# Half of an attention unit's dense products moved ahead of its turning

## The reference

```python
z = h @ w_in[l]
g_a, g_b, z_uv, z_q, z_k, z_v = jnp.split(z, COL_SPLITS, axis=-1)
y_a = gmlp_chunk_mixer(z_uv, ...)
y_b = diff_attention(q, k, v, positions, ...)
m = jax.nn.sigmoid(g_a) * (y_a @ a_w_proj[l]) + jax.nn.sigmoid(g_b) * (y_b @ b_w_proj[l])
x = x + m @ w_out[l]
```

```python
s = jnp.einsum('bhmqd,bhmkd->bhmqk', qb, kb)      # m: two maps per head, 64 features each
p = jax.nn.softmax(jnp.where(mask, s, -jnp.inf), axis=-1)
a = p[:, :, 0] - lam * p[:, :, 1]
o = jnp.einsum('bhqk,bhkd->bhqd', a, vf)
```

## Time and profile before

| | |
|---|---|
| time, median of 3 runs | 1990.88 us (1988.44 to 1991.02) |
| the profiled execution | 1990.19 us, its span 1988.5 us |
| TensorE busy | 1876.0 us, 94% |
| VectorE busy | 1132.6 us, 57% |
| ScalarE busy | 770.1 us, 39% |
| GpSimd busy | 273.7 us, 14% |

### The profile page before, as it was taken

How to read it: one execution, slowest core, us unless ns; L and a number is a source line. 1 busy time by engine, 2 the same in 40 slices (tenths; PEclk the granted TensorE clock), 3 DMA queues, 4 the chain that set the end, 5 groups by cost and what they waited for, 6 DMA issues and landing times.

```text
span 1988.5 us, 22680 instructions
## 1 busy us (share of the span) xinstructions
PE 1876.0 (94%) x8169; PEld 1445.1 (73%) x8169; DVE 1132.6 (57%) x1442; ACT 770.1 (39%) x1081; POOL 273.7 (14%) x246
## 2 busy tenths in 40 slices
PE   6999999989999999998999999897788989999998
PEld 4888888868886767776888888685333768888887
DVE  6556436454655554648767433448998555655532
ACT  4222222233345857214435222334234345445422
POOL 3111001110000000022100000222765300000000
PEclk8999999989999999999999999999998989999999
DMA  5555323333221111224634322342110222232222
GB/s 188 198 173 169 121 64 103 93 111 100 92 85 47 66 59 64 77 93 154 205 127 156 125 76 89 104 122 85 53 53 22 65 80 88 92 98 79 87 87 85
DMA packets 161896, 200.58 MB, mean 101 GB/s; under 512 B 7104, under 2 KB 136490, under 8 KB 161834
## 3 DMA queue, kind: packets, MB, share of 16 engines
q1 hardware_dynamic: 148714, 163.02, 25.6%
q0 software_dynamic: 8672, 28.33, 4.4%
q10 hardware_dynamic: 4448, 8.41, 1.1%
HBM read 189.24 MB, written 10.50 MB: 100 GB/s over the span
## 4 chain that ended last, share of the span: by engine, by line
PE 85%; DVE 10%; ACT 2%; issue 2%; DMA 0%; POOL 0%; DVEq 0%; POOLq 0%; ACTq 0%
PE bank L1671 40%; PE bank L1638 33%; PE bank L1854 6%; DVE sc_a L1520 2%; PE bank L1613 1%; DVE tmp L1028 1%; PE bank L1878 1%; DVE sc_v L1529 1%; PE bank L1650 1%; PE bank L1763 1%; DVE tmp L1541 1%; DVE sc_p L1541 1%; PE bank L2070 1%; DVE sc_p L1540 1%; ACT w_hi L616 0%
## 5 line engine op out<-in xcount | busy, mean ns | idle before, releaser
L1012 DVE TENSOR_TENSOR w_lo<-w_raw,w_hi 128x2048 fp32r<-128x2048 f32 x152 | 359.1, 2362 | 472.5 <-ACT w_hi L616 472.3
L616 ACT CAST w_hi<-w_raw 128x2048 fp32r<-128x2048 f32 x158 | 301.4, 1908 | 752.3 <-PE bank L1638 364.8
L1671 PE MATMUL bank<-h_hi,w_hi 128*128 128x512 f32 x1120 | 448.9, 401 | 35.4 <-ACT h_hi L639 17.6
L1671 PE MATMUL bank<-h_hi,w_lo 128*128 128x512 f32 x1120 | 445.9, 398 | 0.0
L1671 PE MATMUL bank<-h_lo,w_hi 128*128 128x512 f32 x1120 | 355.2, 398 | 0.0
L1671 PEld LDWEIGHTS bank<-h_hi,w_hi 128*128 128x128 f32 x1120 | 212.7, 190 | 90.3 <-issue 38.8
L1671 PEld LDWEIGHTS bank<-h_lo,w_hi 128*128 128x128 f32 x1120 | 212.3, 190 | 51.4
L1671 PEld LDWEIGHTS bank<-h_hi,w_lo 128*128 128x128 f32 x1120 | 212.9, 190 | 50.4 <-issue 0.2
L1638 PE MATMUL bank<-hid_hi,w_lo 128*128 128x512 f32 x528 | 208.8, 396 | 0.0
L1638 PE MATMUL bank<-hid_hi,w_hi 128*128 128x512 f32 x528 | 208.8, 396 | 0.0
L1638 PE MATMUL bank<-hid_lo,w_hi 128*128 128x512 f32 x528 | 208.8, 396 | 0.0
(11 more groups left out here) (368 smaller groups left out, 2644.6 us busy)
## 6 DMA issues: line engine op xcount, KB each, us to landing
w_raw<-in_w_in SPq DMA_DIRECT2D x29, 1024.0 KB, 5.1
mod_raw<-in_w_mod POOLq DMA_DIRECT2D x96, 256.0 KB, 3.6
w_raw<-in_ffn_w_gate SPq DMA_DIRECT2D x22, 1024.0 KB, 7.0
w_raw<-in_ffn_w_up SPq DMA_DIRECT2D x22, 1024.0 KB, 5.4
w_raw<-in_w_up SPq DMA_DIRECT2D x22, 1024.0 KB, 5.1
w_raw<-in_ffn_w_down SPq DMA_DIRECT2D x16, 768.0 KB, 4.7
w_raw<-in_ffn_w_down SPq DMA_DIRECT2D x16, 640.0 KB, 4.3
w_raw<-in_w_out SPq DMA_DIRECT2D x8, 1024.0 KB, 5.1
```

Source lines behind the costliest of these rows:

```text
L616: act.copy(w_hi[i % 2][:], w_raw[i % 2][:]).then_inc(S("w_hi_done"), 1)
L1012: dve.tensor_tensor(w_lo[s][:], w_raw[s][:], w_hi[s][:].bitcast(F32), ALU.subtract).then_inc(S("w_split"), 1)
L1671: mm = pe.matmul(bank[:], w[:, k, at], h[:, k, :], start=k == first and part == 0 and i == 0, stop=k == last and part == 1)
```

## The change

Of the 14 products of a step, seven are taken between `scores(u + 2)` and `weigh(u)`, and seven stay behind `values(u - 1)`. Nothing else is touched; `PER_UNIT` is still 14, and the other engines' lists are the same.

```diff
             for u in range(len(UNITS)):
                 if u + 2 < len(UNITS):
                     scores(u + 2)
+                beside(PER_UNIT // 2)
                 weigh(u)
                 if u:
                     values(u - 1)
-                beside(PER_UNIT)
+                beside(PER_UNIT // 2)
             values(len(UNITS) - 1)
             beside(480 - PER_UNIT * len(UNITS))
```

## The result

The changed kernel takes 1993.53 us (median of 15 runs, 1992.16 to 1994.97), the kernel before 1990.15 us (15 runs, 1988.02 to 1992.43) beside it. The ratio is 1.0018, with a 95% interval of 1.001 to 1.0025: slower by 3.4 us, and by less than 0.2% in the ratio. The prediction was 1993.8 us, from 1989.0 to 1997.3, with 0.73 on "within 0.2%".

The account below looks back on a forecast made before the run. TensorE, busy 94% of the span, was taken to bound the kernel. Waits gone -1.3, new stalls +3.3 and edge +0.9 made +2.9 us: 1993.1 for the profiled execution, 1993.8 against the median, range 1989.0 to 1997.3.

Parts of the forecast that it names:

- the edge: Switch from the mask's short matmuls to a product, 30 times: 0.03 us each, +0.9, with ends -0.9 and +2.4.
- turning of step 22: Step 22's `weigh` waits for VectorE's late weighted difference; products in front cover the wait, -1.14 us.
- turning of step 19: Step 19's `weigh` starts 0.28 us after the mask instead of 0.12; this smaller wait goes, -0.16 us.
- tile 4, step 17: `a_proj` tile starting at product 2 of step 17: its existing stall of 1.09 us grows by 0.37.
- tile 5, step 18: `a_proj` tile starting at product 0 of step 18: its existing stall of 0.34 us grows by 0.70.
- tile 3, step 16: `a_proj` tile starting at product 4 of step 16: new stall of 0.87 us for the multiply freeing its bank.
- tile 1, step 14: `a_proj` tile starting at product 8 of step 14: new stall of about 1.3 us for ScalarE's delayed sigmoid.
- tiles 2 and 6: `a_proj` tiles that come out within 0.1 us of their banks' release; 0.1 us put for both.
- R1: Only step 22's covered stall counts, banks come free early enough: -1.3, 1989.6 us; chance 0.12.
- R2: Each block behind the mask pays its first weight load; decides from 0.067 us a step, 1995.3 at 0.08; chance 0.15.
- R3: Stalls from 692 to 714 us lower TensorE's clock: one fall makes 1995.4 us, two 1997.0; chance 0.08.
- Nothing outside the stretch should move: From step 0's first scores to the last product about 3 us longer; nothing outside that should move.

Follow-up runs that it names:

- products behind the turning: Kernel before, with seven products between `weigh(u)` and `values(u - 1)` and seven behind the values; 1994.74 us in a single run.
- quiet steps: Kernel before, seven products moved ahead of `weigh(u)` only in steps 0 to 12, 20, 21 and 23 to 29, which have no stall; 1989.93 us, single run.
- all 14 ahead: Kernel before, with all 14 products of a step ahead of `weigh(u)` and none behind the values; 2002.87 us in a single run.
- products ahead of the mask: Kernel before, seven products between the scores' four matmuls and the mask's two, in steps 0 to 12, 20, 21, 23 to 29; 1996.28 us, single run.
- emptied first with step 22 split: Kernel before, VectorE's bank-emptying multiplications ahead of `row_max`, and seven products ahead of the turning in step 22 alone; 1987.03 us, ratio 0.9987.
- both engines first: Changed kernel, VectorE's multiplications ahead of `row_max` and ScalarE's sigmoid ahead of the next panel's cast; 1992.26 us, ratio 1.0012.
- before, emptied first: Kernel before, with only VectorE's bank-emptying multiplications moved ahead of `row_max`, TensorE's order unchanged; 1986.44 us, ratio 0.9983.

## Why the prediction was right

Its sum was -1.3 + 3.3 + 0.9 = +2.9 us, and the stretch lost 3.07. The mechanism is borne out term by term; that the sum comes as near as 0.2 us is in part luck, since single terms are off by up to 0.3, upward and downward. Taking the edge of 0.04 out of each step, the terms stand like this:

| term | predicted | from the steps |
|---|---|---|
| turning of step 22 | -1.14 | -1.34 |
| turning of step 19 | -0.16 | -0.20 |
| tile 4, step 17 | +0.37 | +0.40 |
| tile 5, step 18 | +0.70 | +0.72 |
| tile 3, step 16 | +0.87 | +0.94 |
| tile 1, step 14 | +1.3 | +1.18 |
| tiles 2 and 6 | +0.1 | +0.19 (tile 2 alone) |
| the edge, 30 steps | +0.9 (0.03 each) | +1.2 (0.04 each) |

- *The turnings.* Both waits went, and the kernel that splits only steps 19 and 22 shows that they don't return. The size was read from the bracket, 1.14, which counts from the modelled end of the mask matmuls. TensorE's timeline of the kernel before:

```profile
733.43 0.28 PE L1880 MATMUL bank<-mask_parts 128*128 128x128 bf16 x2
734.85 0.55 PE L1889 MATMUL bank<-ident,tmp 128*128 128x128 f32 x3 [1.14 <-DVE tmp L1361]
```

  From the mask to the turning it is 1.42 us where 0.12 is usual, so the wait cost 1.3, as the step's length says.
- *The releases.* That the multiplication is tied to the scores is shown by the reordering on VectorE, which takes all of these waits away, in the old order of TensorE and in the new. That a stall grows by the work that has left the place between scores and tile is borne out by the products behind the turning, where the stalls of tiles 4 and 5 grow less, each by the expected amount and the 0.08 that is not given back.
- *The detour through ScalarE.* A stall in step 14 from a turning in step 13 is shown by splitting step 13 alone. The subtraction of the cast's own wait was needed: without it the stall would have been put at 1.6.
- *The edge* was the term of the sum that was mis-sized, by 0.3 us in all. I started from the values edge, which is free, and put 0.03 where the quiet steps measured 0.04. The Trainium skill ("TensorE: Matmul & The Clock Gate", its part on LDWEIGHTS), with 107 ns for a weight load, gave an estimate of 0.04 a step. But the same account doesn't give the 0.10 behind the scores, nor the nothing behind values and turnings, so that its number fits shows no mechanism; the measurement decides.
- *The rivals.* R1 (only the cover counts) failed at the tiles. R2 (the edge decides) was off: 0.04 where it needed 0.067. R3 (the clock) did not come true: 1.00 was granted from 640 to 790 us, with waits up to 1.50 us. (Its "0.9 to 1.6 us" was a slip: the prediction's own terms make 1.46 at most.) With 3.33 us of waiting the clock did fall, in the run with all 14 ahead.
- *Nothing outside the stretch should move:* behind it nothing did; ahead of it the trace is 0.5 us shorter, within what that part varies from trace to trace.

The loss is 3.4 to 3.6 us by the runs and 3.07 in the stretch of one trace. The difference is within the runs' spread.

## What to carry to other kernels

Before filling a wait with work, add up the waits of that kind in the stretch: here 1.3 us in 170, and the move paid for them in every one of 30 steps. A product that is moved nearer to the start of a step is also moved nearer to the release of its own bank, and a result that is made later holds up whatever stands behind its reader in the reader's queue, a step further on. Where an engine empties a bank that the bound engine waits for, put that ahead of the instruction that itself waits for the bound engine: this one reordering on VectorE gained 0.17%, and the same idea on ScalarE lost, because another engine was waiting for what it pushed back.

## What the hardware showed

- A block of 128x512 products (0.233 us each) starts with a spacing of 0.31 to 0.34 us. After 128x128 fp32 matmuls (turnings or values) these are 0.08 shorter in sum and the block costs nothing; after the bf16 mask pair it costs 0.04 us, after the four fp32 matmuls with 64 rows about 0.10. Why is not shown.
- The idle time in a bracket is too small. It counts from the modelled end of the matmul before, and the first spacing behind a wait is longer (0.31 to 0.34 us for a product instead of 0.233): the turning's 1.14 us cost 1.3, and a wait under 0.2 us (tile 6 in step 18, products behind the turning) shows in no bracket.
- TensorE's clock stayed at 1.00 through waits of 1.50 us (changed kernel) and 2.08 us (all 14 ahead, 725 to 730 us above), and fell to 0.50, its level of 1.2 GHz, behind 3.33 us. Behind the 2.78 us of the kernel with products ahead of the mask it fell too, by its stretches:

```profile
735.00:740.00 5.00, 2.22 (x14) 1.96 (x11) 4.79 (x11) 0.77 (x4) 0.00 (x0) 0.75 0.40 125
740.00:745.00 5.00, 5.00 (x21) 3.52 (x21) 0.08 (x1) 3.20 (x9) 0.00 (x0) 0.91 0.26 89
```

  Two shorter waits close together did it as well. Behind the attention TensorE waits 2.19 and then 2.37 us, with a few transposes between and ahead of them, and in the kernel before its stretches are:

```profile
796.00:798.00 2.00, 0.73 (x4) 0.71 (x4) 2.00 (x4) 0.71 (x2) 0.00 (x0) 0.56 0.37 106
798.00:800.00 2.00, 1.16 (x4) 0.71 (x3) 2.00 (x4) 0.76 (x2) 0.00 (x0) 0.50 1.06 377
```

- Step 0, which begins at a reduced clock, took 5.9 to 6.1 us in nine of the profiled executions and 7.26 to 7.29 in three (products behind the turning; emptied first with step 22 split; both engines first). The second of them has in step 0 the same orders as "before, emptied first", which took 6.00, so a difference of 1.3 us between two single executions can be this alone.
